# Two transformer blocks on one core: a top-score search with its limits and next candidate in a PSUM bank, and steps moved on the engines' queues

## The reference

```python
dots = jnp.einsum('bthd,bsd->bths', iqb, ik).astype(jnp.float32) * idx_scale
score = jnp.einsum('bth,bths->bts', iwb.astype(jnp.float32) * w_scale, jax.nn.relu(dots))
score = jnp.where(admissible[None], score, -jnp.inf)
_, idx = lax.top_k(score, topk)          # topk = 256 of up to 1024 keys, for each query
...
up = jnp.pad(u, ((0, 0), (CONV_K - 1, 0), (0, 0)))      # causal_dwconv3
return up[:, 0:t] * w[0] + up[:, 1:t + 1] * w[1] + up[:, 2:t + 2] * w[2] + b
```

## Time and profile before

| | us |
|---|---|
| median of 3 runs | 2728.93 (2727.0 to 2729.26) |
| the profiled execution | 2729.36 |
| its span | 2727.5 |
| TensorE busy | 2598.9 (95%) |
| VectorE busy | 1322.3 (48%) |
| ScalarE busy | 1035.3 (38%) |
| GpSimd busy | 1232.9 (45%) |
| mean granted clock of TensorE | 0.981 of 2.4 GHz |

### The profile page before, as it was taken

One profiled execution on the slowest core, in us unless ns is written; L12 is line 12 of the kernel. 1 busy time (PEld: TensorE's weight loads), 2 busy tenths in 40 slices (PEclk: granted clock), 3 DMA queues, 4 the chain that ended last, 5 costly groups with the idle time before them and its releaser, 6 DMA issues.

```text
span 2727.5 us, 35270 instructions
## 1 busy us (share of the span) xinstructions
PE 2598.9 (95%) x12632; PEld 2161.0 (79%) x12632; DVE 1322.3 (48%) x2536; ACT 1035.3 (38%) x1928; POOL 1232.9 (45%) x867
## 2 busy tenths in 40 slices
PE   7999999998999999999987999968999999999999
PEld 6878887777888888887866777757887888888887
DVE  4114445277666762225348788557517433333222
ACT  5334553243333332124345566355424333332220
POOL 2132223455666665443414444154236666666442
PEclk9999999999999999999998999989999999999999
DMA  3233212312222244211222111121131322216311
GB/s 130 87 93 90 86 63 102 130 55 90 80 86 78 86 165 159 78 56 49 83 78 66 47 55 63 54 78 33 54 131 59 112 78 85 78 72 253 107 48 70
DMA packets 88684, 236.37 MB, mean 87 GB/s; under 512 B 10144, under 2 KB 22720, under 8 KB 88128
## 3 DMA queue, kind: packets, MB, share of 16 engines
q1 hardware_dynamic: 88512, 234.12, 24.6%
HBM read 178.50 MB, written 51.38 MB: 84 GB/s over the span
## 4 chain that ended last, share of the span: by engine, by line
PE 79%; DVE 7%; issue 3%; ACT 2%; POOL 1%; DMA 1%; SPq 0%; DVEq 0%; ACTq 0%; POOLq 0%
PE PS L887 9%; PE PS L888 9%; PE PS L889 9%; PE PS L643 7%; PE PS L645 7%; PE PS L644 7%; PE PS L905 6%; PE PS L907 6%; PE PS L906 6%; PE PS L769 2%; PE PS L1161 2%; PE PS L744 1%; PE PS L1142 1%; PE PS L857 1%; PE PS L859 1%
## 5 line engine op out<-in xcount | busy, mean ns | idle before, releaser
L643 PE MATMUL PS<-Hh,Wl 128*128 128x512 f32 x1072 | 443.9, 414 | 19.4 <-DVE Hl L1265 11.2
L645 PE MATMUL PS<-Hh,Wh 128*128 128x512 f32 x1072 | 425.2, 397 | 0.0
L644 PE MATMUL PS<-Hl,Wh 128*128 128x512 f32 x1072 | 425.2, 397 | 0.0
L2925 POOL TENSOR_TENSOR Wl<-Wr,Wh 128x1024 fp32r<-128x1024 f32 (+1 forms) x79 | 178.3, 2260 | 430.7 <-ACT Wh L2140 430.7
L3022 POOL TENSOR_TENSOR RG<-RW,RG 128x512 fp32r<-128x512 f32 x176 | 244.2, 1391 | 144.8 <-ACT RG L2401 144.7
L1632 DVE TENSOR_TENSOR XA<-PS,XA 128x512 f32<-128x512 f32 x192 | 132.5, 691 | 333.1 <-PE PS L907 333.1
L905 PE MATMUL PS<-Hh,RG 128*128 128x512 f32 x704 | 274.9, 391 | 1.0 <-POOL Hl L3116 0.6
L907 PE MATMUL PS<-Hh,RG 128*128 128x512 f32 x704 | 274.4, 390 | 0.0
L906 PE MATMUL PS<-Hl,RG 128*128 128x512 f32 x704 | 274.3, 390 | 0.0
L643 PEld LDWEIGHTS PS<-Hh,Wl 128*128 128x128 f32 x1072 | 208.3, 194 | 63.6 <-issue 14.7
L887 PE MATMUL PS<-Hh,RG 128*128 128x512 f32 x640 | 249.2, 389 | 0.0
(11 more groups left out here) (357 smaller groups left out, 5214.4 us busy)
## 6 DMA issues: line engine op xcount, KB each, us to landing
RW<-in_wg SPq DMA_DIRECT2D x44, 512.0 KB, 3.6
RW<-in_wu SPq DMA_DIRECT2D x44, 512.0 KB, 4.5
R<-in_wd SPq DMA_DIRECT2D x88, 256.0 KB, 3.0
hgscr<-GB SPq DMA_DIRECT2D x44, 512.0 KB, 2.6
G<-hgscr SPq DMA_DIRECT2D x40, 512.0 KB, 6.8
Wr<-in_wi SPq DMA_DIRECT2D x23, 512.0 KB, 3.3
Wr<-in_wo SPq DMA_DIRECT2D x16, 512.0 KB, 3.3
spill<-X SPq DMA_DIRECT2D x16, 512.0 KB, 2.6
```

The lines of the kernel that those rows point to most:

```text
L643: pe.matmul(ps(b), k.Wl[:, s, wc], xh[:, kx, sl], start=kk == 0, stop=False)
L644: pe.matmul(ps(b), k.Wh[:, s, wc], xl[:, kx, sl], start=False, stop=False)
L645: i = pe.matmul(ps(b), k.Wh[:, s, wc], xh[:, kx, sl], start=False, stop=kk == nk - 1)
L2925: pool.tensor_tensor(k.Wl[:, s, 0:w], k.Wr[:, s, 0:w], k.Wh[:, s, 0:w].bitcast(F32), ALU.subtract).then_inc(*up("w_lo", "w_lo", u))
```

## The change

The search keeps `least` and a tensor `other` in PSUM bank 6, compares with "less than", and makes the next candidate by one exclusive-or of the shifted result with `other`, which is the candidate with the next bits already changed. That gives three small instructions a bit: the comparison, the candidate, and `other` for the next time. The candidate comes at the end of a bit's last step instead of at the start of the next bit's first. TensorE's first use of bank 6 in the second attention waits for the threshold. Elsewhere:

- the two later taps of `conv_x` become `conv_tap`, called behind columns 2 and 6 of the next product;
- the key split of the next head goes from step 2 to step 4, on ScalarE and GpSimd;
- the gate of row block 3 goes from behind piece (2, 3) plus one to behind piece (3, 5), on all engines that use `DUE`;
- in the output projections `stat` goes from column 2 to column 5, the root from 2 to 6; in the last down tiles `stat` goes from tile (6, 1) to (7, 1), the root behind all tiles, `spread` into the next product, and `row(0)` behind high part 5;
- the last squares of `n1` get slots 2 and 3 of `K1`, and no longer wait for an addition; the additions of tile 7 come ahead of three low parts;
- the two banks of the stage behind the gated addition are used in the order 1, 0.

```diff
-        gate = max(GU[f, 2], GU[f - 1, 3] + 1) if f > 2 else GU[f, 3]
+        gate = GU[f, 3] if f == 2 else GU[f, 5] if f == 3 else max(GU[f, 2], GU[f - 1, 3] + 1)
...
+    def sq_at(tag, kx, n):
+        return n % 2 + 2 * (tag == "n1" and kx == 7)
...
             n = k.sq_no[tag, half, kx]
+            if tag == "n1" and kx == 7:
+                return [("fp", "ffn", NF - 1, 3)]
...
-                later = {(6, 1): {2: lambda: stat(tag, 0)}, (7, 1): {2: lambda: spread(tag, 0)}}.get((m, half), ())
+                later = {(6, 1): {5: lambda: stat(tag, 0)}, (7, 1): {2: lambda: spread(tag, 0)}}.get((m, half), ())
...
-                if nxt and g == 5 and q == 2 and (m, half) == (6, 1):
+                if nxt and g == 5 and q == 2 and (m, half) == (7, 1):
                     stat(nxt, 0)
-                if nxt and g == 5 and q == 2 and (m, half) == (7, 1):
-                    spread(nxt, 0)
...
-                    {2: lambda: stat("ple", 1), 5: lambda: spread("ple", 1)}, fresh=lo("ple"))
+                    {1: lambda: spread("ple", 0), 2: lambda: stat("ple", 1), 5: lambda: spread("ple", 1)}, fresh=lo("ple"))
...
-    bank.of, bank.n = (0, 1), 0
+    bank.of, bank.n = (1, 0), 0
...
+                if r == 0:
+                    pe.wait_ge(*at("thr"))
                 take(6)
...
-        for tap in (1, 0):
-            dve.wait_ge(*at("cv", 1 - tap, j))
-            dve.scalar_tensor_tensor(out=y, in0=k.ZC[:, tap:T + tap], scalar=col("conv_w", 4 * tap + j), in1=y, op0=ALU.mult,
...
+    def conv_tap(j, tap):
+        y = k.YC[:, j % 2, :]
+        dve.wait_ge(*at("cv", 1 - tap, j))
+        dve.scalar_tensor_tensor(out=y, in0=k.ZC[:, tap:T + tap], scalar=col("conv_w", 4 * tap + j), in1=y, op0=ALU.mult,
...
+                taps = {2: lambda j=j: conv_tap(j, 1), 6: lambda j=j: conv_tap(j, 0)} if (c, half) == ("b", 0) else {}
...
-            if nxt and g == 5 and (m, half) == (6, 1):
-                root(nxt, 0)
...
         if nxt:
+            root(nxt, 0)
             for m in range(8):
                 unscaled_low(m, 1)
...
     n1_add(6)
+    n1_add(7)
     for m in range(3):
         n1_low(m, 1)
-    n1_add(7)
...
+    under, least, other = k.sml[:, 264:270].bitcast(I32), ps(6)[:, 0:6], ps(6)[:, 16:22].bitcast(I32)
...
-            prior()
-            if bit == 31:
-                then(dve.memset(cand.bitcast(I32), 0), also=("cand", bit))
-            else:
-                then(dve.scalar_tensor_tensor(out=cand.bitcast(I32), in0=cu, scalar=1 << bit, in1=flip, op0=ALU.bitwise_or,
-                                              op1=ALU.bitwise_xor), also=("cand", bit))
             prior()
             for n in (3, 2, 1, 0):
...
-            then(dve.tensor_tensor(over, cnt, least, ALU.is_ge))
-            prior()
...
-                then(dve.tensor_scalar(kb, over, float(1 << bit), None, ALU.mult))
-                prior()
-                then(dve.tensor_tensor(cu, cu, kb, ALU.bitwise_or))
+                then(dve.tensor_tensor(under, cnt, least, ALU.is_lt))
+                prior()
+                then(dve.scalar_tensor_tensor(out=ci if bit else kb, in0=under, scalar=bit, in1=other if bit else ci,
+                                              op0=ALU.logical_shift_left, op1=ALU.bitwise_xor),
+                     also=("cand", bit - 1) if bit else None)
+            prior()
+            if bit > 1:
+                then(dve.tensor_scalar(other, ci, 1 << (bit - 2), None, ALU.bitwise_xor))
+            elif bit:
+                then(dve.tensor_copy(other, ci))
             yield
...
-        if i == 2 and h < 7:
+        if i == 4 and h < 7:
             key_high(h + 1)
...
-                    later = {2: lambda: root(tag, 0)}
+                    later = {6: lambda: root(tag, 0)}
...
         if nxt:
+            root(nxt, 0)
             for m in range(8):
                 unscaled_high(m, 1)
-                if m == 3:
+                if m == 5:
                     row(0)
```

More of the change, by code:

```diff
@@ L1200, in add @@
         dve.wait_ge(*at("acc", tag, half, k_ - 1))
-        dve.tensor_tensor(k.acc[:, sl], k.acc[:, sl], k.K1[:, n % 2, :], ALU.add).then_inc(
+        dve.tensor_tensor(k.acc[:, sl], k.acc[:, sl], k.K1[:, k.sq_at(tag, k_, n), :], ALU.add).then_inc(
             *up("add", "acc", tag, half, k_, also=("acc", tag, half) if k_ == k.last[tag] else None))
@@ L1398, in conv_x @@
             *up("conv", "cv", 0, j))
-        for tap in (1, 0):
-            dve.wait_ge(*at("cv", 1 - tap, j))
-            dve.scalar_tensor_tensor(out=y, in0=k.ZC[:, tap:T + tap], scalar=col("conv_w", 4 * tap + j), in1=y, op0=ALU.mult,
-                                     op1=ALU.add).then_inc(*up("conv", "cv", 2 - tap, j))
+    def conv_tap(j, tap):
+        y = k.YC[:, j % 2, :]
+        dve.wait_ge(*at("cv", 1 - tap, j))
+        dve.scalar_tensor_tensor(out=y, in0=k.ZC[:, tap:T + tap], scalar=col("conv_w", 4 * tap + j), in1=y, op0=ALU.mult,
+                                 op1=ALU.add).then_inc(*up("conv", "cv", 2 - tap, j))
     def y1_low(half):
@@ L1420, in vector @@
             for half in range(2):
-                walk(8, 3 if (c, j) == ("b", 3) else 2, {}, tick)
+                taps = {2: lambda j=j: conv_tap(j, 1), 6: lambda j=j: conv_tap(j, 0)} if (c, half) == ("b", 0) else {}
+                walk(8, 3 if (c, j) == ("b", 3) else 2, taps, tick)
                 b = bank.next()
@@ L1805, in vector @@
     bg.drain()
-    cu, xm, kb = (k.sml[:, a:a + 6].bitcast(I32) for a in (32, 38, 56))
-    cand, cnt, thr, over, least = (k.sml[:, a:a + 6] for a in (44, 50, 64, 256, 264))
-    flip = k.sml[:, 272:278].bitcast(I32)
+    kb = k.sml[:, 56:62].bitcast(I32)
+    cand, cnt, thr, over = (k.sml[:, a:a + 6] for a in (44, 50, 64, 256))
+    under, least, other = k.sml[:, 264:270].bitcast(I32), ps(6)[:, 0:6], ps(6)[:, 16:22].bitcast(I32)
     fix = k.sml[:, 280:288]
@@ L1827, in count @@
                                    accum_out=out))
-        then(dve.memset(cu, 0))
-        then(dve.memset(xm, -1))
+        then(dve.memset(cand.bitcast(I32), 0), also=("cand", 31))
         then(dve.memset(least[:, 0:4], 255.5))
@@ L1850, in topk @@
             prior()
-            then(dve.tensor_tensor(over, cnt, least, ALU.is_ge))
-            prior()
             if bit == 31:
-                then(dve.tensor_scalar(kb, over, -2147483648.0, None, ALU.mult))
+                then(dve.tensor_tensor(over, cnt, least, ALU.is_ge))
                 prior()
-                then(dve.tensor_copy(cu, kb))
-                then(dve.tensor_scalar(xm, over, -2147483647.0 - 1.0, None, ALU.mult))
-                prior(1)
                 then(dve.tensor_scalar(kb, over, 1.0, None, ALU.subtract))
                 prior()
-                then(dve.tensor_tensor(xm, xm, kb, ALU.bitwise_or))
+                then(dve.tensor_scalar(ci[:, 4:6], kb[:, 4:6], -(1 << 30), None, ALU.bitwise_xor))
+                then(dve.tensor_scalar(ci[:, 0:4], kb[:, 0:4], 1 << 30, None, ALU.bitwise_xor), also=("cand", bit - 1))
+            else:
+                then(dve.tensor_tensor(under, cnt, least, ALU.is_lt))
                 prior()
-                then(dve.tensor_copy(flip[:, 0:4], xm[:, 0:4]))
-                then(dve.tensor_scalar(flip[:, 4:6], xm[:, 4:6], -(1 << 31), None, ALU.bitwise_xor))
-            else:
-                then(dve.tensor_scalar(kb, over, float(1 << bit), None, ALU.mult))
-                prior()
-                then(dve.tensor_tensor(cu, cu, kb, ALU.bitwise_or))
+                then(dve.scalar_tensor_tensor(out=ci if bit else kb, in0=under, scalar=bit, in1=other if bit else ci,
[6 more added lines that the diff above has]
+                then(dve.tensor_copy(other, ci))
             yield
+        then(dve.tensor_copy(thr[:, 0:4].bitcast(I32), kb[:, 0:4]))
+        then(dve.tensor_scalar(thr[:, 4:6].bitcast(I32), kb[:, 4:6], -(1 << 31), None, ALU.bitwise_xor))
         prior()
-        then(dve.tensor_tensor(thr.bitcast(I32), cu, xm, ALU.bitwise_xor))
         yield
@@ L2163, in square @@
             act.wait_ge(*at(*e))
-        act.activation(k.K1[:, n % 2, :], src, ACT.Square).then_inc(*up("sq", "sq", tag, half, k_))
+        act.activation(k.K1[:, k.sq_at(tag, k_, n), :], src, ACT.Square).then_inc(*up("sq", "sq", tag, half, k_))
     def root(tag, half):
@@ L2549, in feed_forward @@
             if nxt and g == 5:
-                if (m, half) == (6, 1):
-                    root(nxt, 0)
                 if (m, half) == (3, 0):
```

4 lines of the change are left out of this document (3 added, 1 removed).

## The result

The changed kernel takes 2682.39 us (median of 4, 2680.51 to 2687.02; the profiled execution 2683.16) against 2727.97 us beside it (median of 4): a ratio of 0.9836, 95% interval 0.9819 to 0.9853, 45.6 us less. The forecast was 2684.

The account below looks back on a forecast made before the run. TensorE bounds the kernel, busy 2598.9 of 2727.5 us. Search 21, attention 10, gate 5.5, projections 0.5, last down tiles 3.2 and first norm 4.5 sum to 44.7, so 2728.9 becomes 2684; range 2674 to 2698, with two rivals 2668 to 2706.

Parts of the forecast that it names:

- The search: Search beside retention: three small instructions a bit, each with a bank operand, no longer held behind GpSimd; 21 us gained.
- the waits at L1058: Three TensorE waits, 8.0 us, for SD queued on VectorE behind held small instructions; 7 us plus 3 of clock gained.
- L1090: TensorE's 10.5 us wait for ScalarE's late last copy falls to 1.1, the copy alone; 9.4 us plus 1.8 of clock.
- rival 1: Whole kernel: new waits on hidden transfers and chains take part; only search and gate pay, 2702 us; chance 0.17.
- Clock: TensorE's matmuls run slower after longer pauses; shorter pauses return time, 8.8 us over all terms.
- Attention: First block's attention beside the convolution: moving taps and key split removes waits at L758 and L744; 10 us gained.
- The gate: Row block 3: running conv3(3,0) after v(3) and c22(3) leaves 2.5 us of a 7.0 us wait; 5.5 us gained.
- the last down tiles: Later statistics leave 0.9 of a 3.67 us wait, with 0.6 new at the spread; 3.2 us gained with clock.
- The first norm: Block two: own slots and earlier additions make half 0's sum ready sooner; 4.5 us gained, the bank swap adding nothing.
- 2 (still held): Search: VectorE's three instructions stay held behind GpSimd, so it gives about 5 instead of 21 us; 2700; chance 0.07.
- 3 (slower): Search: small instructions with a bank operand queue behind other PSUM traffic, at 2.3 us each 2829 us; chance 0.02.
- 4 (no difference from the search): Search: step lengths are set by ScalarE's counts, so no gain there; the rest pays in part, 2715 us; chance 0.04.

Follow-up runs that it names:

- e1: The kernel before with the search's part of the change alone (bank 6, three small instructions, early candidate, TensorE's wait for the threshold): 2708.64 us, ratio 0.9931.
- e2: The changed kernel with the search as before, all other parts kept: 2705.31 us, ratio 0.9918.
- e5: The changed kernel with the two banks behind the gated addition back in the old order 0, 1: 2682.54 us, ratio 0.9835.
- e7: The changed kernel with the two later convolution taps back behind the first, key split kept at step 4: 2686.29 us, ratio 0.9850.
- e8: The changed kernel with the key split back at step 2, the taps kept apart: 2688.68 us, ratio 0.9862.
- e9: The changed kernel with the gate of row block 3 back behind piece (2, 3) plus one: 2688.68 us, ratio 0.9863.
- e12: The changed kernel with half 0's additions first and the second half of row block 2's convolution behind v(3): 2679.06 us, ratio 0.9826.
- e4: The changed kernel with its three small search instructions, but least counts and other candidate in SBUF instead of bank 6: 2698.60 us, ratio 0.9897.
- e6: The changed kernel with block two's first norm's last squares in old slots and additions in old order, banks still swapped: 2686.80 us, ratio 0.9851.
- e10: The changed kernel with the statistics of the output projections and last down tiles at their old places: 2688.55 us, ratio 0.9867.
- e11: The changed kernel with half 0's last two additions ahead of the lows and half 1's additions in block two's first norm: 2679.84 us, ratio 0.9831.
- e3: The kernel before with its four small search instructions kept, each given one operand in bank 6, plus TensorE's threshold wait: 2711.22 us, ratio 0.9942.

## Why the prediction was right

- **The search** (21 forecast; 20.2 by the traces of e1, 20.9 by those of e2, 23.1 by the table). Its ground held: bank operands end the holding. The third form, the one that writes a bank, was priced at its lower bound of 0.166 us and measured 0.167 to 0.169.
- **Within that sum two terms were off, in opposite ways, and that they cancel is luck.** For the waits at L1058 the forecast took 7 us of waits and 3 of clock; by the traces the three places give 13.7, the whole 8.0 and 5.7 of clock, 1.9 behind each. For L1090 it took 9.4 us of wait and 1.8 of clock, 11.2; e1 gives 6.2. The step that failed was that "the three later rounds wait there ... 1.1 us, the copy alone", hence a gain of 9.4. What is late next at the first round is not the copy. ScalarE's, GpSimd's and TensorE's timelines of the changed kernel:

```profile
...
1466.99 0.60 ACT L2647 ACTIVATE rr<-PS 128x512 f32<-128x512 f32 x1 [5.87 <-POOL KR L3173]
...
```

```profile
...
1458.42 1.31 POOL L3173 TENSOR_TENSOR KR<-rr,CS 128x512 f32<-128x512 f32 x1
1462.90 1.30 POOL L3177 TENSOR_TENSOR K<-K,CS 128x512 f32<-128x512 f32 x1 [3.17 <-DMA K<-rr]
1464.28 1.30 POOL L3179 TENSOR_TENSOR KR<-KR,K 128x512 f32<-128x512 f32 x1
1465.53 1.29 POOL L3173 TENSOR_TENSOR KR<-rr,CS 128x512 f32<-128x512 f32 x1
...
```

```profile
...
1470.46 0.74 PE L1096 MATMUL PS<-mats,rr 128*128 128x128 f32 x5 [2.29 <-ACT rr L2647]
```

ScalarE's copy is released by GpSimd's L3173, whose predecessor L3177 sat 3.17 us for a transfer. The wait of 2.29 us also looks better than it is. TensorE comes to it late, since the matmuls just ahead of the stretch run slower in this trace than in e5's. The windows of 5 us at their start, of the changed kernel and of e5, in the columns of the earlier trace rows:

```profile
...
1432.50:1437.50 5.00, 4.91 (x12) 3.90 (x13) 4.72 (x5) 2.92 (x4) 1.16 (x1) 0.52 0.57 210
...
```

```profile
...
1430.00:1435.00 5.00, 4.84 (x21) 4.04 (x22) 4.72 (x5) 3.00 (x4) 1.09 (x1) 1.00 0.58 210
...
```

The runs with the search's three instructions fall in two groups. Where these matmuls run at 1.2 GHz (the changed kernel, e7, e8, e9, e12) the wait is 2.3 to 3.5 us; where they run at 2.4 GHz (e1, e4, e5, e6, e10, e11) it is 4.6 to 5.1. Counted from the matmul at 1432.59 (L989) the wait ends after 37.9 to 39.0 us in all of them, after 39.5 in e3, and after 43.9 and 44.2 in the kernel before and e2. So the search's part brought this point some 6 us forward, and the chain through GpSimd holds it there, at whichever clock TensorE got to it. That is rival 1's ground in small, a chain with more than one late link. But it takes nothing from the earlier parts: e1 has none of them and still waits 4.9 us.
- **Clock.** Forecast 8.8 us over all terms, measured 12.4. The search's windows were named: 0.83 or 0.93 became 1.00 at three places. The forecast took 3 us for the three at SD, though its own row had 1.7 for one and its bound was 5.1; 5.7 is where the sum was short. Behind L758 some 1.3 us came back, and 1.2 at the gate.
- **Attention** (10, measured 11.7). The 1.6 us set aside for held taps weren't needed: even behind the worst held tap, 3.43 us, TensorE has no wait. The split, by e7 and e8, is 4.8 and 6.8.
- **The gate** (5.5, measured 5.7 and 5.6 in e9): 2.60 us were left of 7.03, "2.5 stay".
- **The projections** (0.5 for both, measured 0.5 for each in e10) **and the last down tiles** (3.2, measured 2.9): waits of 0.98 us (0.9 forecast) and 1.15 us at the spread (0.6 forecast).
- **The first norm** (4.5, measured 2.8 to 3.9) was short too. The step took the third addition between the undisturbed 1372.5 and the held 1374.9 and put 4.5 us. The held case came, which gives 3.5. GpSimd's piece returned every 4.65 us there (1342.26, 1346.90, 1351.55), so the held case was the likely one. That the swap adds nothing of its own is shown by e5. The sign named for it, the sum at L659 down from 12.3 to about 7, didn't come: it is 9.3. With the banks swapped TensorE no longer waits 2.5 us for the bank and so waits as long as before, 6.2 us, for the statistics.
- **Rivals.** 2 (still held) fell with a maximum of 0.169 us in 91 instructions, and e4 shows what it would have cost: 16.2 us, where it was put at 16. 3 (slower) would have needed over 1 us each. 4 (no difference from the search) fell with e1 and e2. 1 is there only as the wait of some 5 us that stays at L1090 and the 1.15 us at the spread.
- **The sum.** Terms add. By the traces, and each in its own stretches, the parts taken out of the changed kernel are worth 4.8 us (e7), 6.8 (e8), 5.6 (e9), 5.2 (e10), 3.9 (e6) and 20.9 (e2), together 47.2; the whole, from 180 us on, is 47.4.
- **The range.** The terms' lower bounds add up to 22 us (10, 4, 4, 0.5, 0 and 3.5), which is 2707, so the slow end of 2698 doesn't follow from them; the fast end, 2674, does.

## What to carry to other kernels

Where VectorE works on a handful of elements beside GpSimd, look at the spread of durations, not the mean: a median of 0.17 us with a maximum of 2.3 is an instruction that waits for another engine's whole piece, and one operand in a PSUM bank ended it here (15 of 18 us), while the shorter step was worth 3 more (7 where the operands stayed in SBUF). Price a shortened wait by asking what releases it next on every engine in its chain, GpSimd and transfers included. A pause of TensorE costs its own length and, for those of 2.5 to 4.3 us here, mostly 1.3 to 1.9 us of slower matmuls behind it, once some 3 (e10). And a wait that is short in one profile may be short because the waiting engine came late: measure from a fixed point to its end.

## What the runs showed of the hardware

- **A small VectorE instruction costs the same from a bank as from SBUF.** 0.161 to 0.169 us with one operand in a bank, input or output (the changed kernel), 0.166 to 0.171 with none when it is not held (e4). The same four instructions have medians of 0.162, 0.168, 0.161 and 0.161 us in e3, with a bank operand, and of 0.167, 0.172, 0.166 and 0.156 in the kernel before, without. The Trainium skill's page "VectorE: DVE Perf Modes", section on the TRN2 errata, has 62 cycles more for a PSUM source, as an estimate 0.065 us for each. These rows don't show that, and they decide here.
- **The same matmuls at either clock.** In the index stage the changed kernel and e5 have nearly the same wait, and the two matmuls behind it take 1.10 us in one and 2.05 us in the other, at 2.4 and at 1.2 GHz:

```profile
...
1418.47 1.10 PE L1025 MATMUL PS<-CT,wkv 128*128 128x512 f32 x2 [2.13 <-DVE CT L1262]
...
```

```profile
...
1413.66 2.05 PE L1025 MATMUL PS<-CT,wkv 128*128 128x512 f32 x2 [2.27 <-DVE CT L1262]
...
```

It is so in all fourteen traces: this pair takes 1.10 us in seven and 2.05 in the other seven. No edit lies near, and what decides it isn't shown. So a single profile can be 2 us off in such a stage, and the first 180 us, which no edit touches, take from 3.2 us less to 2.7 us more in the twelve experiments' profiles than in the changed kernel's.
